# The transposed x tiles, hi and lo, placed 32 bytes further along in SBUF

## What is computed

```
x = x + 0.5 * swiglu(rms_norm(x, g1), w_in, w_out)
u = rms_norm(x, g2) @ w_mix_in          # and the mixer on the pieces of u
x = x + mixed @ w_mix_out
x = x + 0.5 * swiglu(rms_norm(x, g3), w_in, w_out)
# swiglu: a, b = split(x @ w_in, 2); (silu(a) * b) @ w_out, D_FF = 2816
```

## The kernel before

| tile | start | modulo 512 | modulo 128 | modulo 64 |
|---|---|---|---|---|
| raw, hi, lo | 16512, 41088, 65664 | 128 | 0 | 0 |
| params | 106624 | 128 | 0 | 0 |
| xT_hi, xT_lo | 110912, 119104 | 320 | 64 | 0 |
| memT_hi, memT_lo | 151872, 160064 | 320 | 64 | 0 |
| br_hi (three), br_lo | 168256 and on | 320 | 64 | 0 |
| hT_hi, hT_lo | 192832, 194880 | 320 | 64 | 0 |
| gw_hi, gw_lo (weights of 24 gates) | 215360, 216128 | 320, 64 | 64 | 0 |
| cmp_hi, cmp_lo (first pair) | 182464, 184384 | 192, 64 | 64 | 0 |

## Time and profile before

### The profile page before, as it was taken

One profiled execution on the slowest core, in us unless ns is written; L12 is line 12 of the kernel. 1 busy time (PEld: TensorE's weight loads), 2 busy tenths in 40 slices (PEclk: granted clock), 3 DMA queues, 4 the chain that ended last, 5 costly groups with the idle time before them and its releaser, 6 DMA issues.

```text
span 1827.3 us, 33276 instructions
## 1 busy us (share of the span) xinstructions
PE 1790.4 (98%) x13114; PEld 1656.0 (91%) x13114; DVE 1060.1 (58%) x1393; ACT 911.7 (50%) x1180; POOL 45.3 (2%) x66
## 2 busy tenths in 40 slices
PE   8999998999999999999999999999999999999998
PEld 8999877999999999888898999899999888989997
DVE  5554686645464556666676544555464657675454
ACT  5444565443344445476755444443454567644443
POOL 0000120000000000000000000000000000000000
PEclk9999999999999999999999999999999999999999
DMA  7555423555465555443354555555546442445552
GB/s 311 203 188 189 176 108 116 207 199 191 170 241 189 201 184 190 179 164 136 136 188 162 196 184 178 210 201 190 185 158 232 165 181 94 162 150 208 193 197 93
DMA packets 47856, 329.19 MB, mean 180 GB/s; under 512 B 5392, under 2 KB 5648, under 8 KB 9616
## 3 DMA queue, kind: packets, MB, share of 16 engines
q1 hardware_dynamic: 44496, 316.84, 47.9%
q10 hardware_dynamic: 3264, 11.03, 1.8%
HBM read 326.80 MB, written 1.05 MB: 179 GB/s over the span
## 4 chain that ended last, share of the span: by engine, by line
issue 82%; PE 13%; ACT 2%; POOL 1%; DVE 1%; DMA 0%; DVEq 0%; POOLq 0%; ACTq 0%
PE work L1496 3%; PE work L1495 3%; PE work L1497 3%; POOL rstd L552 1%; PE acc L1497 1%; PE acc L1495 1%; PE acc L1496 1%; DMA pre<-pre 0%; ACT prob L720 0%; PE acc L1588 0%; PE work L1554 0%; DVE lo L1003 0%; ACT hi L601 0%; ACT squared L621 0%; PE acc L1714 0%
## 5 line engine op out<-in xcount | busy, mean ns | idle before, releaser
L1003 DVE TENSOR_TENSOR lo<-raw,hi 128x2048 fp32r<-128x2048 f32 x280 | 640.0, 2292 | 468.2 <-ACT hi L601 467.8
L1495 PE MATMUL work<-xT_hi,hi 128*128 128x256 f32 x2752 | 768.1, 279 | 6.8 <-DVE lo L1003 6.4
L1497 PE MATMUL work<-xT_hi,lo 128*128 128x256 f32 x2752 | 763.7, 277 | 0.0
L1496 PE MATMUL work<-xT_lo,hi 128*128 128x256 f32 x2752 | 763.6, 277 | 0.0
L601 ACT ACTIVATE hi<-raw 128x2048 fp32r<-128x2048 f32 x280 | 534.2, 1911 | 233.8 <-PE work L1497 191.2
L1495 PEld LDWEIGHTS work<-xT_hi,hi 128*128 128x128 f32 x2752 | 518.8, 189 | 17.3 <-DVE lo L1003 8.2
L1496 PEld LDWEIGHTS work<-xT_lo,hi 128*128 128x128 f32 x2752 | 519.0, 189 | 2.5
L1497 PEld LDWEIGHTS work<-xT_hi,lo 128*128 128x128 f32 x2752 | 518.6, 188 | 0.0
L1497 PE MATMUL acc<-hi,hT_lo 128*128 128x512 f32 x480 | 189.2, 394 | 0.0
L1496 PE MATMUL acc<-lo,hT_hi 128*128 128x512 f32 x480 | 188.3, 392 | 0.0
L1495 PE MATMUL acc<-hi,hT_hi 128*128 128x512 f32 x480 | 187.1, 390 | 0.0
(11 more groups left out here) (262 smaller groups left out, 1944.4 us busy)
## 6 DMA issues: line engine op xcount, KB each, us to landing
raw<-stream SPq DMA_DIRECT2D x298, 1024.0 KB, 4.8
pre<-pre ACTq DMA_DIRECT2D x7, 512.0 KB, 5.8
mem_in<-mem ACTq DMA_DIRECT2D x3, 1024.0 KB, 5.8
post<-post ACTq DMA_DIRECT2D x6, 512.0 KB, 3.8
x<-x SPq DMA_DIRECT2D x2, 512.0 KB, 5.1
pre<-pre SPq DMA_DIRECT2D x2, 512.0 KB, 3.7
out<-x SPq DMA_DIRECT2D x4, 256.0 KB, 2.0
alibi<-alibi ACTq DMA_DIRECT2D x1, 768.0 KB, 15.3
```

What stands on the lines that cost most here:

```text
L1003: nc.vector.tensor_tensor(lo[:, s, :], raw[:, s, :], hi[:, s, :].bitcast(F32), ALU.subtract).then_inc(lo_ready, 1)
L1495: nc.tensor.matmul(dst, a_hi, b_hi, start=start, stop=False)
L1496: nc.tensor.matmul(dst, a_hi, b_lo, start=False, stop=False)
L1497: return nc.tensor.matmul(dst, a_lo, b_hi, start=False, stop=stop)
```

## The change

Ahead of the two tiles 32 bytes are left free, and behind them 480, so that they start 32 bytes later and all that follows starts 512 bytes later.

```diff
         params = new("params", [P, max(B1P_N, LP_N)])
+        room(32)
         xT_hi = new("xT_hi", [P, KD, T], F32R)
         xT_lo = new("xT_lo", [P, KD, T], F32R)
+        room(480)
         pre = new("pre", [P, D])
```

## The result

| | before | changed |
|---|---|---|
| median, us | 1825.63 | 1858.49 |
| lowest to highest | 1823.98 to 1831.79 | 1857.17 to 1858.97 |
| span of the profiled execution | 1827.3 | 1856.2 |

Measured in turn on one chip, the changed kernel takes 1.0172 times as long, with a 95% interval of 1.0153 to 1.019. The medians are 32.9 us apart. The forecast was 1860.6.

The account below looks back on a forecast made before the run. TensorE was taken as the bound, with its moving-operand read just short of full clock. Adding 34 us for moving xT and 0 for all else to 1829.4 gave 1863.4, or 1860.6 us at the median; range 1806 to 1868.

Parts of the forecast that it names:

- TensorE's pace is the time: Whole kernel: TensorE is busy 98% of the span, so what one matmul costs it is what the kernel costs.
- The moving xT term, 7,690 x 4.4 = 34 us: Matmuls with xT moving: nine tenths of 8,544 go to the slow pace, 4.4 ns more each, 34 us; chance 0.38.
- mean of 277 ns: L1495 xT records, between 276 and 281 ns: read as 10 to 30% slow already; one in ten was used.
- xT as stationary operand, 0 and at most 1.3 us: 288 loads of xT beside 512-column matmuls: no cost expected, at most 288 x 4.4 ns = 1.3 us.
- the load is covered twice over: xT as stationary operand: loads of 188 ns beside matmuls 230 ns apart, so cost 0.
- Gaps and tiles behind, 0; writing the tiles, 0: Gaps issue nothing, tiles behind keep their remainder modulo 512, and ScalarE and VectorE pieces writing xT cost the same: 0.
- The length of the weight load is not the cause: The 6.6 ns stall per xT matmul: loads of 24 columns instead of 128 still gave 114.3 ns.
- each reads at 32 modulo 64 unharmed: Gate product: every second weight load starts at 32 modulo 64, yet the mean is still 114.3 ns.
- br and memT stay.: Matmul groups over br and memT: expected to stay as they were while the three xT groups carry the difference.
- nothing happens: Rival for the moving read: its start may not matter, so the time stays at 1827 us; chance 0.36.
- Faster: Rival: 32 bytes remove part of the 6.6 ns stall, 1812 or 1808 us, to 1781 at most; chance 0.18.
- A full extra unit: Rival: each moving xT piece covers 17 units of 64 bytes instead of 16, + 61 us, 1887 us; chance 0.08.

Follow-up runs that it names:

- e9: xT moved by 256 bytes against the kernel before, other tiles keeping their remainder modulo 512; 1827.53 us, ratio 0.9994.
- e4: Kernel before plus 24 bursts of 40 unused xT matmuls, with varied moving and stationary starts and weight-load lengths; one run, 1961.07 us.
- e3: xT moved by 64 bytes against the kernel before, other tiles keeping their remainder modulo 512; 1873.26 us, ratio 1.0225.
- e1: All tiles, xT and weights alike, moved 32 bytes further against the kernel before; 1827.11 us, ratio 0.9984.
- e2: Only the weight tiles hi and lo moved by 32 bytes against the kernel before, xT left; 1865.11 us, ratio 1.0185.
- e8: Kernel before plus 45 bursts of 32 unused matmuls, each offset entered behind 1, 2 and 3 short plain float32 matmuls; one run, 2114.78 us.
- e10: Kernel before with hT tiles 64 bytes further and 1 to 4 short plain float32 matmuls ahead of FFN xT stretches from the third chunk; 1850.62 us, ratio 1.0122.
- e12: Kernel before with hT 64 bytes further, two short float32r matmuls ahead of xT stretches in the first block's FFNs, three in others; 1846.26 us, ratio 1.0079.

## Why the prediction was right

The time came out 2.1 us below the forecast, and the range, the sign and the mechanism held. By its steps:

- **TensorE's pace is the time.** Right: distances that begin with a moving xT grew by 33.0 us, the rest of the balance is -3.8 us, and no other engine has more to do.
- **The moving xT term, 7,690 x 4.4 = 34 us.** Its size is right, its two factors are not. The forecast took the slow pace of the trace, 117.7 ns, for the nine tenths that were fast. What came is a pace that the kernel before does not have, 118.3 ns, for all of them, the formerly slow first chunks included: 5.0 ns for those that were fast and 0.5 for the others. Nor were quite nine tenths fast. Of whole stretches one tenth ran slow, as it said, but of all triples only 84% took 344 ns or less, since those at the head of a stretch are slow too. (Its reading "mean of 277 ns" left out the first of the three lines, with 279.) The plain distances cost 36.3 us, more than forecast, and shorter waits within the stretches gave 3.5 us back. That the sum, 33.0 / 8,544 = 3.9 ns each, meets the forecast's 4.0 is in part luck.
- **xT as stationary operand, 0 and at most 1.3 us.** The upper bound came: 229 to 233 ns, 1.2 us. The step that failed is "the load is covered twice over". Its length is covered, its start is not: a load of 188 ns beside matmuls 229 ns apart still delays them.
- **Gaps and tiles behind, 0; writing the tiles, 0.** Right. e9 has the tiles behind at the same addresses as the changed kernel and costs nothing, and the pieces that write the tiles take what they took: 597 ns on ScalarE, 687 and 685 on VectorE.
- **"The length of the weight load is not the cause" and "each reads at 32 modulo 64 unharmed".** The rows stand, and the product is at 114.6 ns in the changed kernel too. The inference does not hold in general: with 24 columns of `hi` the same read takes 116.6 and 117.8, with 64 columns 119.0 and 116.7 (e4), and the gate product itself takes 116.0 with xT 64 bytes on (e3). It carried no term, only a part of the chance for no change.
- **"br and memT stay."** memT does. br became faster, 1.5 us, by falling into the other of its two paces. Its own addresses kept their difference, so that it was handed on by what stands ahead is likely, but no run shows it for br.

Of the rivals, *nothing happens* leant on the argument that the two reads sweep past each other anyway, so that no start can matter. e1 and e2 refute it: a change of the difference of the two starts costs, whichever of them moves, and moving both costs nothing. Its other support, in the Trainium skill, "SBUF — State Buffer", section "Specifications (TRN2)", with lines of 16 bytes, fails as well: a shift of exactly 16 costs 5.9 ns (e4). The Trainium skill, "SBUF — State Buffer", section "Who interferes with whom", calls TensorE's two read ports independent and says that it never waits on anyone. Against that these runs measure a matmul that takes up to 8.6 ns more than 113.3 by the starts of its own two operands (121.9, e4). That the two reads meet at the memory is the likeliest reading of this; no row shows the ports. That TensorE waits for no other engine at the SBUF is not contradicted by any run.

*Faster* had its own good ground: a better distance does exist, but for the matmuls of 512 columns (226.7 ns at distance 0), not for those of 256. Of the places that were tried, xT was at its best already. *A full extra unit*, 120 ns, came true for a shift of 64 bytes (e3), where no such unit is cut, so its reason was wrong.

**What stays open.** Why 192 is the good distance for 256 moving columns and 0 for 512, why a load of 64 columns turns the order round, and what has a period of 256 bytes, no run tells. What chooses between 113.3 and 117.8 is shown to be what stands ahead (e8, e10 to e12), but not by which rule; in e9 identical code took both. The distance of `br` and `memT` was not changed by itself.

## What to carry to other kernels

When TensorE is the bound and each matmul has its own weight load, read the distances between starts to the nanosecond and compare them with columns over the clock: here 6% of a matmul (113.3 to 120.0 ns) hung on the difference of two tile starts modulo 256 bytes, and moving one operand by 32 bytes without the other cost 1.7% of the kernel (xT) and 1.9% (the weights). Move all operands together or by multiples of 256 bytes (shown here for weight loads of 128 columns), and after any change of addresses look at stretches that the change did not touch, since a stretch can hand its pace to the next. A gap of a few bytes issues nothing and can still cost.

## What was not expected of the hardware

- The distances between matmuls settle into repeating patterns: 113.3 or 117.8 ns for 256 columns at the good distance; 118.3 (as 116, 116, 120, 117, 122, 118, 116, 122) at 32 bytes off; 120.0 at 64; 117.8 at 128, and there once 113.4. The same data, instructions and clock give any of them.
- One operand of three out of step costs more than all three: 37.9 us against 33.0.
- A better place for one tile (hT, -3.7 us) made its neighbours slower by 22.4 us, and one float32r matmul of 32 columns ahead of each stretch gave 13.7 us of it back; three did not free a loop.
- A plain float32 matmul of 256 columns leaves two records 216 ns apart, so it takes four cycles a column and not the two that the prediction read from the earlier trace rows, where each record was taken for a matmul. For it an offset of 32 or 64 bytes changes nothing.
- To go from float32r to plain float32 takes some 92 ns beyond the matmul's own time, and back some 95 (318 against 226 and 126 against 31, e10).
